# Block one's attention scores: from half-array fp32 products to whole-array fp32r products with high and low parts

## The chip, the cores and the metric

The kernel runs on one core of one Trainium2 chip. The metric is the device time of one execution in microseconds. Engines are named as in the profile: PE is TensorE (PEld its loads of the stationary operand), DVE is VectorE, ACT is ScalarE, POOL is GpSimd and SP issues most transfers.

## The reference, cut to what matters

The program is two transformer-like layers over 256 tokens of width 1024. Block one holds a sparse attention with 8 query heads of width 64, which share 2 key heads (4 query heads each). Each query head is scored three times: against 15 compressed keys, against the keys k_s of the selection branch, and against the keys k_w of the window branch.

```python
q = rms_norm(q.reshape(B_, S_, N_HEADS, HEAD_DIM), q_norm_g)
k_s = rms_norm(k_s.reshape(kv_shape), k_norm_g[1])
k_w = rms_norm(k_w.reshape(kv_shape), k_norm_g[2])
kc = rms_norm(compress(k_c.reshape(kv_shape), cmp_pos_k, w_cmp_k), k_norm_g[0])
...
s_c = (jnp.einsum('bsgrd,bcgd->bgrsc', q, kc) * SCALE - slopes * dist_c)      # compressed: 15 keys
...
s = (jnp.einsum('bqgrd,bgqmd->bgrqm', q_i, ks) * SCALE - slopes * dist)        # selection
s = (jnp.einsum('bqgrd,bkgd->bgrqk', q_i, k_i) * SCALE - slopes * dist)        # window
```

(The einsum texts are shortened; each is the product of one head's queries with its group's keys over the 64 head dimensions.) With 256 tokens the selection takes all blocks and the window reaches over all of them, so both branches are causal attention over all 256 keys with different keys and values.

## The kernel before, in words

Every large product is made from weights that are split in two: ACT writes the high part of a loaded unit of weights (2 k-tiles of 128x512, tile `whi`, type fp32r), DVE subtracts it from the loaded fp32 values and writes the low part (`wlo`, line 1787). PE adds three products per tile: high by high, high by low, low by high. Units follow one another in a fixed order (`b1_q`, `b1_kv`, `b1_w`, `b1_c0`, `b1_x0`, `b1_c1`, `b1_x1`, ...), and a ring of five buffers lies between the engines. The groups c0, x0, c1, x1 feed the convolution branch; their four tiles each are written by PE in banks 0 to 3, the left halves copied by ACT and the right halves added by DVE (`add_right`, line 2129, out `CC` or `UU`). Tile f of a group uses the same bank as tile f of the group before, so PE waits with the first product of tile f (`wait_bank`) for DVE's `add_right` of tile f in the group before.

Attention of block one is a side program, written as a generator on PE, ACT and DVE. Each engine takes one step `s` of it per unit, from the first unit of `b1_c0` on. The order on each engine is fixed by this text; nothing is scheduled otherwise.

- Step 1 to 3 on PE: the keys to be compressed (n = 0), the queries (n = 1, 2) and the keys k_s and k_w (n = 3) are turned into banks 4 and 5, head dimension on rows, two heads of 64 rows each.
- ACT copies them with their gains into `TT` (12 tiles of 128x256; steps 2 to 4). POOL then moves the keys by two transfers each so that each key head is there in both halves of the rows (`kc_swapped`, `ks_swapped`).
- DVE adds the position embedding into `KP` (steps 3 and 4), PE compresses the keys (step 5), ACT, DVE and POOL norm them (steps 6 and 7) and DVE writes them into `KCT`.
- Step 7 on PE: eight fp32 products give the compressed scores: 128 rows (two query heads, with zeros in `KCT` where head and key don't belong together) by 64 columns. DVE adds the bias (`CB`) to them in step 8.
- Steps 10, 13, 16, 19, 22, 26, 29, 32 on PE (`pair_at`): a pair is two query heads and one branch. The two heads stand in rows 0 to 63 and 64 to 127, so each product uses 64 rows of the array, and the two heads' products go to banks 4 and 5. Queries 0 to 127 meet 128 keys, queries 128 to 255 meet 256 keys: four fp32 instructions a pair. DVE (`negated`) takes the scores from there.

The lines of the trace: 523 is every product of PE, 527 every turn, 1174 every copy of ACT, 2010 `KP`, 2016 to 2029 the norm of the compressed keys, 2041 the bias.

## Time and profile before

| | us |
|---|---|
| median of 3 runs | 902.2 (902.16 to 902.3) |
| profiled execution | 901.26 |
| its span | 899.2 |
| PE busy | 892.7 (99%) |
| DVE busy | 706.0 (79%) |
| ACT busy | 555.3 (62%) |

The granted clock of PE was 0.999 of full speed in the profiled execution. PE is busy from end to end: the chain of work that ended last is PE for 99% of the span. A busy time of PE is made of overlapping records, so the price of a piece of PE's work is read from one start to the next start behind it. fp32 instructions leave two records each (two passes), fp32r instructions and turns one; the profile prints both types as f32.

### The profile page before, as it was taken

The numbers are of one execution on the slowest core, as the hardware profiler recorded it, in microseconds if no ns is written. First come the engines' busy times: TensorE is split into PE (matmuls) and PEld (weight loads), VectorE is DVE, ScalarE is ACT, GpSimd is POOL, SyncE is SP. The second block draws the span as 40 slices with busy tenths as digits, with TensorE's granted clock in tenths as the row PEclk, the third lists the DMA queues.
The fourth block names the chain that finished last, engine by engine and source line by source line (L and its number), as shares of the span: only waits on it lengthen the run. The fifth ranks groups of instructions, "written<-read, shape, count | busy, mean of one in ns | idle before, by whom it ended". The sixth has DMA issues, their size and how long they took to land.

```text
span 899.2 us, 13582 instructions
## 1 busy us (share of the span) xinstructions
PE 892.7 (99%) x4926; PEld 767.0 (85%) x4926; DVE 706.0 (79%) x1381; ACT 555.3 (62%) x954; POOL 43.2 (5%) x54
## 2 busy tenths in 40 slices
PE   9999999999999999999999999999999999999997
PEld 7988877888888888888889998888889988888886
DVE  6888899789866666677998999999976786666665
ACT  7767878755644444456655657776745755754454
POOL 0410000000000000000010100100000000000000
PEclk9999999999999999999999999999999999999999
DMA  9977677676465555556798888487565377555551
GB/s 343 320 214 199 177 203 219 198 293 202 154 229 187 192 191 196 190 191 209 219 236 268 231 206 270 106 230 240 169 211 164 114 212 237 187 187 187 188 188 47
DMA packets 97218, 184.53 MB, mean 205 GB/s; under 512 B 8128, under 2 KB 18176, under 8 KB 96896
## 3 DMA queue, kind: packets, MB, share of 16 engines
q1 hardware_dynamic: 92128, 166.35, 56.1%
q0 software_dynamic: 4656, 16.78, 10.0%
q8 instruction: 40, 0.66, 0.3%
q10 hardware_dynamic: 368, 0.52, 0.2%
q14 instruction: 26, 0.21, 0.1%
HBM read 164.69 MB, written 1.05 MB: 184 GB/s over the span
## 4 chain that ended last, share of the span: by engine, by line
PE 99%; ACT 1%; issue 0%; DVE 0%; DVEq 0%; ACTq 0%
PE pb L523 97%; PE pb L527 1%; PE pb L738 1%; ACT SM L1400 0%; ACT wlo L1174 0%; ACT SM L1174 0%; ACT whi L1174 0%; ACT PTC L1174 0%; DVE XS L2617 0%; DVE XS L2625 0%; DVEq L59 0%; DVE DG L2359 0%; ACT MSQ L1757 0%; DVE ST L2603 0%; ACT CC L1174 0%
## 5 line engine op out<-in xcount | busy, mean ns | idle before, releaser
L1174 ACT ACTIVATE whi<-raw 128x1024 fp32r<-128x1024 f32 (+2 forms) x304 | 309.1, 1039 | 125.5 <-PE pb L523 112.5
L1787 DVE TENSOR_TENSOR wlo<-raw,whi 128x1024 fp32r<-128x1024 f32 (+1 forms) x267 | 315.7, 1211 | 78.7 <-ACT whi L1174 78.2
L523 PE MATMUL pb<-XT,whi 128*128 128x512 f32 (+1 forms) x1232 | 283.8, 358 | 0.0
L523 PE MATMUL pb<-whi,ZO 128*128 128x512 f32 (+1 forms) x776 | 238.9, 388 | 0.0
L523 PEld LDWEIGHTS pb<-XT,whi 128*128 128x128 f32 x1232 | 200.8, 189 | 23.8 <-issue 1.4
L523 PEld LDWEIGHTS pb<-whi,ZO 128*128 128x128 f32 x776 | 145.2, 188 | 29.7 <-issue 0.4
L523 PE MATMUL pb<-XT,wlo 128*128 128x256 f32 (+1 forms) x1032 | 166.4, 282 | 0.0
L523 PEld LDWEIGHTS pb<-XT,wlo 128*128 128x128 f32 (+1 forms) x1032 | 153.2, 190 | 14.0
L523 PE MATMUL pb<-whi,XT 128*128 128x512 f32 (+1 forms) x544 | 161.8, 389 | 0.0
L523 PE MATMUL pb<-wlo,ZO 128*128 128x512 f32 (+1 forms) x388 | 148.3, 387 | 0.0
L523 PEld LDWEIGHTS pb<-whi,XT 128*128 128x128 f32 x544 | 101.0, 188 | 20.7 <-issue 0.7
L523 PE MATMUL pb<-wlo,XT 128*128 128x512 f32 (+1 forms) x272 | 95.8, 384 | 0.0
L2291 DVE SCALAR_TENSOR_TENSOR YC<-U,PR,YC 128x255 f32<-128x255 f32 (+14 forms) x240 | 94.9, 462 | 0.0
L523 PEld LDWEIGHTS pb<-wlo,ZO 128*128 128x128 f32 x388 | 72.9, 188 | 14.3
L2186 DVE TENSOR_TENSOR HF<-pb,RT 128x256 f32<-128x256 f32 x64 | 26.8, 419 | 43.1 <-ACT RT L1174 43.1
L523 PEld LDWEIGHTS pb<-wlo,XT 128*128 128x128 f32 x272 | 51.1, 188 | 9.8
L1174 ACT ACTIVATE RT<-pb 128x256 f32<-128x256 f32 x64 | 22.5, 374 | 55.0 <-PE pb L523 55.0
L1174 ACT ACTIVATE ZO<-HF 128x256 fp32r<-128x256 f32 x64 | 26.8, 418 | 31.1 <-DVE HF L2189 29.4
L1174 ACT ACTIVATE wlo<-raw 128x1024 fp32r<-128x1024 f32 x31 | 32.7, 1055 | 13.5 <-PE pb L523 13.5
L2664 POOL DMA_DIRECT2D wlo<-raw x31 | 26.9, 867 | 289.3 <-ACT wlo L1174 289.3
L2071 DVE STREAM_TRANSPOSE PT<-SM 32x192 f32<-32x192 f32 x80 | 29.5, 369 | 1.1
L2189 DVE SCALAR_TENSOR_TENSOR HF<-HF 128x256 f32<-128x256 f32 x64 | 27.2, 425 | 2.2
(258 smaller groups left out, 657.9 us busy)
## 6 DMA issues: line engine op xcount, KB each, us to landing
raw<-in_w_in SPq DMA_DIRECT2D x105, 512.0 KB, 4.8
raw<-in_w_ff SPq DMA_DIRECT2D x64, 512.0 KB, 5.3
raw<-in_w_up SPq DMA_DIRECT2D x32, 512.0 KB, 4.5
raw<-in_w_down SPq DMA_DIRECT2D x32, 512.0 KB, 4.8
wlo<-raw POOLq DMA_DIRECT2D x31, 512.0 KB, 5.8
raw<-in_w_branch_b SPq DMA_DIRECT2D x8, 512.0 KB, 5.3
raw<-in_w_out SPq DMA_DIRECT2D x8, 512.0 KB, 4.1
raw<-in_wx_kv SPq DMA_DIRECT2D x8, 512.0 KB, 5.4
```

Of the source, the lines that this page charges most:

```text
L523: return e.matmul(o, l, r, start=start, stop=stop, skip_group_check=True)
L527: return e.transpose(o, s, ident[0:n, 0:n])
L738: i = e.matmul(PB[4 + j][:, k * 256 + t * P:k * 256 + t * P + P], src[:, c:c + P], ident, start=k + t == 0, stop=k + t == 2, is_transpose= ...
L1174: return e.activation(o, i, ACT.Copy, scale=scale)
L1787: e.tensor_tensor(wlo[u % NW][:, 0:c], raw_tile(u)[:, 0:c], whi[u % NW][:, 0:c].bitcast(F32), ALU.subtract).then_inc(lo, 1)
L2071: i = e.transpose(PT2[n % 2][b:b + 32, :, a:a + 32], SM2[n % 2][a:a + 32, :, b:b + 32])
L2186: e.tensor_tensor(HF[:, f, :], PB[bank_of[name, f]][:, 0:256], RT[:, m % 2, :], ALU.add).then_inc(out_d, 1)
L2189: e.scalar_tensor_tensor(out=HF[:, f, :], in0=HF[:, f, :], scalar=0.0, in1=HF[:, f, :], op0=ALU.max, op1=ALU.mult).then_inc(h_sq, 1)
L2291: m = e.scalar_tensor_tensor(out=y, in0=U2[:, f, 30:256 + k], scalar=prm("convw2", 8 * k + f), in1=y, op0=ALU.mult, op1=ALU.add)
L2664: e.dma_start(wlo[u % NW][:, 0:c].bitcast(F32), raw_tile(u)[:, 0:c], accum_op=ALU.add).then_inc(lo_summed[u % NW], 16)
```

## The change

Each head's queries are kept as a high part (fp32r) in one half of the rows and their low part in the other half, 128 rows in all, in the columns of `OT` (`q_cols`, the right half of tile `ZO`; written there before attention's outputs come). The keys' high parts stand in both halves of the rows (`k_cols(g, 0, b)`), and so do their low parts (`k_cols(g, 1, b)`). A head's scores are then two fp32r products over all 128 rows, one with the keys' high part and one with their low part; all four partial products are summed. For this

- ACT's copies (n = 1 to 3) are made by halves of 64 rows: 12 instead of 6;
- DVE makes the low parts (`qk_low`, a new function, 4 instructions each in steps 3, 4 and 5), reading banks 4 and 5 again;
- PE's turn of n = 3 waits for `qk_low(1)`, which reads the bank that it writes;
- POOL moves the keys after `qk_low(3)`, by 2 transfers of 256 KB (`ks_doubled`) instead of 2 of 128 KB;
- a pair is 8 fp32r instructions instead of 4 fp32 ones;
- the compressed keys are treated alike (`KCS`): 16 fp32r products of 32 columns (16 high, 16 low) instead of 8 fp32 ones of 64 columns; DVE writes two tiles in step 7 and adds both products to the bias, which is loaded straight into `PC`, by 8 small instructions instead of 2 in step 8. The zeroing of `KCT` on POOL is gone.

Left out below: semaphore names, tile sizes and the zeroing.

```diff
...
+
+KCS = ZT[:, 0:64]
+
+def q_cols(f, p):
+    return slice(512 * f + 256 * p, 512 * f + 256 * p + 256)
+
+def k_cols(g, l, b):
+    a = 2048 + 1024 * g + 512 * l + 256 * b
+    return slice(a, a + 256)
...
-TQ, TK, TC = 0, 4, 8
-
-def key_tile(first_tile, w, g, half):
-    return first_tile + w + 2 * (g != half)
+def qk_gain(n, j, r):
+    a = PRM["kg"] + 1 + j
+    return PR[r, a:a + 1] if n == 3 else QG[r, 2 * n - 2 + j:2 * n - 1 + j]
+
+def key_tile(w, g, half):
+    return w + 2 * (g != half)
...
-            e.dma_start(CB[:, :], A["consts2"]).then_inc(cb_in, 16)
+            e.dma_start(PC[:, :], A["consts2"][:, 0:512]).then_inc(cb_in, 16)
+            e.dma_start(CB[:, 512:1024], A["consts2"][:, 512:1024]).then_inc(cb_in, 16)
         if u == b1 + 51:
...
-                    e.wait_ge(qk_out, n - 1)
+                    e.wait_ge(*((kc_copied, 1) if n == 2 else (qk_lo, 1)))
                 for j in range(2):
...
-                e.wait_ge(qk_out, 3)
+                e.wait_ge(qk_lo, 2)
+                kcs = KCS.rearrange("p (l n) -> p l n", l=2)
                 for t in range(2):
...
-                        a = 256 * t + 64 * f
-                        i = mm(PB[7][:, a:a + 64], TT[:, TQ + f, t * P:t * P + P], KCT[:, :],
-                               t == 0 and f == 0, t == 1 and f == 3)
+                        for p in range(2):
+                            a, g = 256 * t + 64 * f + 32 * p, f // 2
+                            i = mm(PB[7][:, a:a + 32].rearrange("p (l n) -> p l n", l=2),
+                                   OT[:, q_cols(f, p)][:, t * P:t * P + P], kcs[:, :, 15 * g:15 * g + 16],
+                                   a == 0, a == 480)
                 i.then_inc(cs_done, 1)
...
-                f, k = n // 2, [key_tile(TK, n % 2, n // 4, p) for p in range(2)]
-                e.wait_ge(qk_out, 4)
-                e.wait_ge(ks_swapped, 32)
+                f, b, g = n // 2, n % 2, n // 4
+                e.wait_ge(qk_lo, 3)
+                e.wait_ge(ks_doubled, 32)
                 if n:
...
-                    r = slice(64 * p, 64 * p + 64)
-                    mm(PB[4 + p][:, 0:128], TT[r, TQ + f, 0:128], TT[r, k[p], 0:128], True, False)
-                for p in range(2):
-                    r = slice(64 * p, 64 * p + 64)
-                    mm(PB[4 + p][:, 128:384], TT[r, TQ + f, 128:256], TT[r, k[p], 0:256], False,
+                    q = OT[:, q_cols(f, p)]
+                    mm(PB[4 + p][:, 0:128], q[:, 0:128], OT[:, k_cols(g, 0, b)][:, 0:128], True, False)
+                    mm(PB[4 + p][:, 0:128], q[:, 0:128], OT[:, k_cols(g, 1, b)][:, 0:128], False, False)
+                    mm(PB[4 + p][:, 128:384], q[:, 128:256], OT[:, k_cols(g, 0, b)], False, False)
+                    mm(PB[4 + p][:, 128:384], q[:, 128:256], OT[:, k_cols(g, 1, b)], False,
                        True).then_inc(sc_done, 1)
...
-                i0 = (TC, TQ, TQ + 2, TK)[n]
                 e.wait_ge(qk_t, n + 1)
...
-                    copy(TT[:, i0:i0 + 2, :].rearrange("p i n -> p (i n)"), PB[4][:, :]).then_inc(qk_out, 1)
-                else:
-                    if n < 3:
-                        e.wait_ge(qg_made, 1)
-                    g = [prm("kg", 1 + j) if n == 3 else QG[:, i0 + j - TQ:i0 + j - TQ + 1] for j in range(2)]
-                    copy(TT[:, i0, :], PB[4 + n % 2][:, 0:256], g[0])
-                    copy(TT[:, i0 + 1, :], PB[4 + n % 2][:, 256:512], g[1]).then_inc(qk_out, 1)
+                    copy(TT[:, 0:2, :].rearrange("p i n -> p (i n)"), PB[4][:, :]).then_inc(kc_copied, 1)
+                    continue
+                if n < 3:
+                    e.wait_ge(qg_made, 1)
+                for j in range(2):
+                    for p in range(2):
+                        r = slice(64 * p, 64 * p + 64)
+                        o = OT[r, q_cols(2 * n - 2 + j, p) if n < 3 else k_cols(p, 0, j)]
+                        i = copy(o, PB[4 + n % 2][r, 256 * j:256 * j + 256], qk_gain(n, j, r))
+                i.then_inc(qk_hi, 1)
             if s == 6:
...
-                e.wait_ge(kc_zero, 3)
+                e.wait_ge(kc_zero, 2)
                 step(copy(KC[0:30, 0:64], PB[7][0:30, 0:64]))
...
+    def qk_low(n):
+        e.wait_ge(qk_hi, n)
+        for j in range(2):
+            for p in range(2):
+                r, q = slice(64 * p, 64 * p + 64), slice(64 - 64 * p, 128 - 64 * p)
+                c = q_cols(2 * n - 2 + j, p) if n < 3 else k_cols(p, 0, j)
+                o = OT[q, c] if n < 3 else OT[r, k_cols(p, 1, j)]
+                i = e.scalar_tensor_tensor(out=o, in0=PB[4 + n % 2][r, 256 * j:256 * j + 256],
+                                           scalar=qk_gain(n, j, r), in1=OT[r, c].bitcast(F32),
+                                           op0=ALU.mult, op1=ALU.subtract)
+        i.then_inc(qk_lo, 1)
+
     def attention1():
...
+            if s in (3, 4, 5):
+                qk_low(s - 2)
             if s in (3, 4):
-                e.wait_ge(*((qk_out, 1) if s == 3 else (kc_swapped, 32)))
+                e.wait_ge(*((kc_copied, 1) if s == 3 else (kc_swapped, 32)))
                 for w in range(2):
...
-                        v = TT[r, key_tile(TC, w, g, half), 16 * half:16 * half + 240].rearrange(
+                        v = TT[r, key_tile(w, g, half), 16 * half:16 * half + 240].rearrange(
                             "p (c j) -> p c j", j=16)
...
-                e.wait_ge(kc_zero, 3)
+                e.wait_ge(kc_zero, 2)
                 step(e.tensor_scalar(KCN[0:30, :].rearrange("p (q d) -> p q d", q=2),
...
-                    i = e.transpose(KCT[32 * b:32 * b + 32, 32 * (b // 2):32 * (b // 2) + 32],
-                                    KCN[0:32, 32 * b:32 * b + 32])
+                    i = e.transpose(KCT[32 * b:32 * b + 32, :], KCN[0:32, 32 * b:32 * b + 32])
                 step(i)
...
-                e.tensor_scalar(KCT[:, :], KCT[:, :], prm("kg"), None, ALU.mult).then_inc(kct_out, 1)
+                step(e.tensor_scalar(KCS[:, 0:32], KCT[:, :], prm("kg"), None, ALU.mult))
+                after_step()
+                e.scalar_tensor_tensor(out=KCS[:, 32:64], in0=KCT[:, :], scalar=prm("kg"),
+                                       in1=KCS[:, 0:32].bitcast(F32), op0=ALU.mult,
+                                       op1=ALU.subtract).then_inc(kct_out, 1)
             pcv = PC[:, :].rearrange("p (h n) -> p h n", n=32)
...
-                e.wait_ge(cb_in, 16)
-                for p in range(2):
-                    d = PC[:, :].rearrange("p (t q n) -> p t q n", t=2, q=2)[:, :, p, :]
-                    b = CB[:, 0:512].rearrange("p (t q n) -> p t q n", t=2, q=2)[:, :, p, :]
-                    step(e.tensor_tensor(
-                        d.rearrange("p t (f n) -> p t f n", f=4),
-                        PB[7][:, :].rearrange("p (t f q n) -> p t f q n", t=2, f=4, q=2)[:, :, :, p, :],
-                        b.rearrange("p t (f n) -> p t f n", f=4), ALU.add))
+                e.wait_ge(cb_in, 32)
+                pc = PC[:, :].rearrange("p (t q f n) -> p t q f n", t=2, q=2, f=4)
+                cs = PB[7][:, :].rearrange("p (t f q l n) -> p t f q l n", t=2, f=4, q=2, l=2)
+                for l in range(2):
+                    if l:
+                        after_step()
+                    for g in range(2):
+                        for q in range(2):
+                            d = pc[:, :, q, 2 * g:2 * g + 2, 15 * g:15 * g + 15]
+                            step(e.tensor_tensor(d, cs[:, :, 2 * g:2 * g + 2, q, l, 0:15], d, ALU.add))
                 after_step()
...
-    for n, i, done in ((1, TC, kc_swapped), (4, TK, ks_swapped)):
-        e.wait_ge(qk_out, n)
-        e.dma_start(TT[64:128, i + 2:i + 4, :], TT[0:64, i:i + 2, :]).then_inc(done, 16)
-        e.dma_start(TT[0:64, i + 2:i + 4, :], TT[64:128, i:i + 2, :]).then_inc(done, 16)
+    e.wait_ge(kc_copied, 1)
+    e.dma_start(TT[64:128, 2:4, :], TT[0:64, 0:2, :]).then_inc(kc_swapped, 16)
+    e.dma_start(TT[0:64, 2:4, :], TT[64:128, 0:2, :]).then_inc(kc_swapped, 16)
+    e.wait_ge(qk_lo, 3)
+    for g in range(2):
+        r, q = slice(64 * g, 64 * g + 64), slice(64 - 64 * g, 128 - 64 * g)
+        k = OT[:, 2048 + 1024 * g:3072 + 1024 * g].bitcast(F32)
+        e.dma_start(k[q, :], k[r, :]).then_inc(ks_doubled, 16)
     e.wait_ge(kc_mean, 1)
...
```

DVE around step 3, before the change and after (`ZO` is the tile with the high and low parts, `KP` the keys with their positions, `CC` the right halves of group c0; line 2017 of the changed kernel is `qk_low`):

```order
L1787 TENSOR_TENSOR wlo<-raw,whi 128x1024 [waits w_hi_made] x2
L2010 TENSOR_TENSOR KP<-TT,PR 64x240 [waits qk_copied]
L2010 TENSOR_TENSOR KP<-TT,PR 64x240 x3
L2129 TENSOR_TENSOR CC<-pb,CC 128x256 [waits left_halves_copied] x4
L1787 TENSOR_TENSOR wlo<-raw,whi 128x1024 [waits w_hi_made]
```

```order
L1804 TENSOR_TENSOR wlo<-raw,whi 128x1024 [waits w_hi_made] x2
L2017 SCALAR_TENSOR_TENSOR ZO<-pb,ST,ZO 64x256 [waits qk_hi_made]
L2017 SCALAR_TENSOR_TENSOR ZO<-pb,ST,ZO 64x256 x3
L2041 TENSOR_TENSOR KP<-TT,PR 64x240 [waits cmp_keys_copied]
L2041 TENSOR_TENSOR KP<-TT,PR 64x240 x3
L2165 TENSOR_TENSOR CC<-pb,CC 128x256 [waits left_halves_copied] x4
L1804 TENSOR_TENSOR wlo<-raw,whi 128x1024 [waits w_hi_made]
```

Four instructions stand now ahead of `KP` and of the four `add_right` of c0.

PE at the first pair (step 10), before the change and after (`TT` and `ZO` hold queries and keys; `XT` and `wlo`, `whi` belong to the main stream):

```order
L523 MATMUL pb<-XT,wlo 128x256 x7
L523 MATMUL pb<-TT 128x128 [waits keys_swapped,qk_copied]
L523 MATMUL pb<-TT 128x128
L523 MATMUL pb<-TT 128x256 x2
L523 MATMUL pb<-XT,whi 128x512 [waits turned_lo,w_lo_made,w_hi_made]
```

```order
L535 MATMUL pb<-XT,wlo 128x256 x7
L535 MATMUL pb<-ZO 128x128 [waits keys_doubled,qk_lo_made]
L535 MATMUL pb<-ZO 128x128
L535 MATMUL pb<-ZO 128x256 x2
L535 MATMUL pb<-ZO 128x128 x2
L535 MATMUL pb<-ZO 128x256 x2
L535 MATMUL pb<-XT,whi 128x512 [waits turned_lo,w_lo_made,w_hi_made]
```

The place in the stream is the same; four instructions on two half arrays became eight on the whole array.

## Rows read from the trace of the kernel before

**Rows 1.** The page: PE's busy time; shares of the chain that ended last, by engine.

```profile
PE 892.7 (99%) x4926; PEld 767.0 (85%) x4926; DVE 706.0 (79%) x1381; ACT 555.3 (62%) x954; POOL 43.2 (5%) x54
...
PE 99%; ACT 1%; issue 0%; DVE 0%; DVEq 0%; ACTq 0%
```

**Rows 2.** Window 40:50: length; busy PE, PEld, DVE, ACT, POOL; clock, DMA share, GB/s.

```profile
40.00:50.00 10.00, 10.00 (x65) 8.97 (x64) 8.95 (x16) 7.59 (x15) 1.97 (x4) 1.00 0.89 281
```

**Rows 3.** Timeline of PE, 42 to 44 us: start, duration, line, operation, count.

```profile
42.59 1.11 PE L523 MATMUL pb<-XT,wlo 128*128 128x256 f32 x8
43.54 0.60 PE L527 MATMUL pb<-CST,QKV 128*128 128x128 f32 x4
```

**Rows 4.** Timeline of PE, steps 3 to 8 of attention.

```profile
46.78 0.60 PE L527 MATMUL pb<-CST,QKV 128*128 128x128 f32 x4
47.14 0.71 PE L523 MATMUL pb<-XT,whi 128*128 128x512 f32 x2
...
52.88 2.01 PE L523 MATMUL pb<-WC,KP 128*30 128x64 f32 x64
...
60.51 1.90 PE L523 MATMUL pb<-KCT,TT 128*128 128x64 f32 x16
62.21 0.71 PE L523 MATMUL pb<-XT,whi 128*128 128x512 f32 x2
```

**Rows 5.** Timeline of PE around the first pair.

```profile
69.72 1.11 PE L523 MATMUL pb<-XT,wlo 128*128 128x256 f32 x8
70.77 0.93 PE L523 MATMUL pb<-TT 64*128 64x128 f32 x8
71.62 0.72 PE L523 MATMUL pb<-XT,whi 128*128 128x512 f32 x2
72.19 0.40 PE L523 MATMUL pb<-XT,wlo 128*128 128x256 f32 x2
```

**Rows 6.** Timeline of PE: an fp32 product of 256 columns over 128 rows.

```profile
24.93 0.59 PE L523 MATMUL pb<-DR,CST 128*128 128x256 f32 x2
...
25.60 0.40 PE L523 MATMUL pb<-wlo,XT 128*128 128x512 f32 x1
```

**Rows 7.** Timeline of DVE, 41 to 74 us.

```profile
41.86 2.35 DVE L1787 TENSOR_TENSOR wlo<-raw,whi 128x1024 fp32r<-128x1024 f32 x2
44.13 1.65 DVE L2010 TENSOR_TENSOR KP<-TT,PR 64x240 f32<-64x240 f32 x4
45.79 1.33 DVE L2129 TENSOR_TENSOR CC<-pb,CC 128x256 f32<-128x256 f32 x3
...
48.35 1.23 DVE L1787 TENSOR_TENSOR wlo<-raw,whi 128x1024 fp32r<-128x1024 f32 x1 [0.52 <-ACT whi L1174]
...
55.56 0.14 DVE L2016 TENSOR_SCALAR ST<-ST 30x1 f32<-30x1 f32 x1 [1.34 <-ACT KCN L1366]
...
57.71 0.26 DVE L2029 TENSOR_SCALAR KCT<-KCT,PR 128x64 f32<-128x64 f32 x1
...
59.13 0.43 DVE L2129 TENSOR_TENSOR UU<-pb,UU 128x256 f32<-128x256 f32 x1 [0.82 <-ACT UU L1174]
...
63.45 0.75 DVE L2041 TENSOR_TENSOR PC<-pb,CB 128x256 f32<-128x256 f32 x2
...
69.94 0.18 DVE L2059 TENSOR_TENSOR ST<-ST 128x16 f32<-128x16 f32 x1
...
73.10 0.42 DVE L2129 TENSOR_TENSOR CC<-pb,CC 128x256 f32<-128x256 f32 x1
```

**Rows 8.** Timeline of DVE: two low parts of 128x256.

```profile
12.35 0.88 DVE L2365 SCALAR_TENSOR_TENSOR XT<-XG,XT 128x256 fp32r<-128x256 f32 x2
```

**Rows 9.** Timeline of ACT: query copies and the next high part.

```profile
41.01 0.83 ACT L1174 ACTIVATE TT<-pb,ST 128x256 f32<-128x256 f32 x2
41.73 1.07 ACT L1174 ACTIVATE whi<-raw 128x1024 fp32r<-128x1024 f32 x1
```

**Rows 10.** Timeline of PE: the first tile of x1.

```profile
74.51 0.63 PE L523 MATMUL pb<-XT,whi 128*128 128x512 f32 x2
```

## What is predicted

> **What bounds the kernel now.** I read the page first: PE is busy for 892.7 of 899.2 us and makes 99% of the chain that ended last [rows 1]. So the time is PE's own work, and the change is worth what it takes from PE's stream less each wait that it puts into it. ACT and DVE cost nothing until PE waits for them. The windows show where that is near: from 40 to 50 us, where the queries and keys are copied, DVE is busy 8.95 of 10 us [rows 2], and the change gives DVE more work just there. So I read PE's timeline for the price of each product by the distance of starts, then DVE's timeline for the slack between its work and PE's waits.
>
> **PE, the pairs.** Before, a pair takes 70.77 to 71.62 = 0.85 us. The group ahead of it (eight products of 256 columns) takes 69.72 to 70.77 = 1.05, while the same group ahead of a turn takes 42.59 to 43.54 = 0.95, so entering a pair costs 0.10 more. Behind it the first two products of 512 columns take 71.62 to 72.19 = 0.57, where four times 0.119 (a price worked out below) would be 0.48, so leaving it costs 0.1 [rows 3, 5]. Together 0.95 a pair, and 1.05 where the main stream follows at once, which it does behind the first pair.
>
> The new pair is eight whole-array fp32r products: four of 256 columns, at 0.95/8 = 0.119 each [rows 3], and four of 128 columns. No row shows an fp32r product under 256 columns. Bounds: the compressed scores are 16 passes of 64 columns in 60.51 to 62.21, so 0.106 each [rows 4]. Their columns are few, so this is the price of loading 128 stationary columns; each new product needs such a load as well. On the other side, an fp32 product of 256 columns and the 512-column product behind it take 24.93 to 25.60 = 0.67 [rows 6]; less 0.23 for the latter (the eight products at the fp32r pace of 0.119 per 256 columns give it) that is 0.44, or 0.22 for 128 columns at the fp32 rate. Below, a product of 128 columns that costs by its columns alone would take some 0.06, half of 0.119. I take 0.107, since the compressed scores are the nearest row: many passes, few columns, all 128 rows. A pair is then 4 x 0.119 + 4 x 0.107 = 0.90, with no entry cost since the array is used as by its neighbours. Eight pairs save 8 x 0.05 plus 0.1 at the first: **-0.5 us**. With 0.22 a pair is 1.36 and the eight cost 8 x 0.41 - 0.1 = +3.2; with 0.06 a pair is 0.72 and they save 8 x 0.23 + 0.1 = 1.9.
>
> What the pairs give up is that two heads run beside each other on half arrays. The Trainium skill, page "TensorE: Matmul & The Clock Gate", section "LDWEIGHTS (loading the stationary operand)", says that a load takes as long as it has columns, whatever its rows: 107 ns for 128 by its formula. By that rule, the trace agrees. Its section "Back-to-back issue gap" gives some 81 ns for a sustained product of 128 columns with its load; by that a pair would be 0.80 and the pairs would save 1.3 in place of 0.5, which is an estimate from that page. The 0.106 of the row speaks against it, and I go by the row.
>
> **PE, the compressed scores.** Eight fp32 products leave 16 passes of 0.106; 16 fp32r products of 32 columns need 16 loads too. At the price of a load: **0**. If few columns made them cheap (0.06), -0.7; even at the fp32 rate 32 columns stay below 0.106.
>
> **ACT.** Six copies of 128x256 become twelve of 64x256; the number of columns is the same, so each costs what one costs now, about 0.36 from start to start (41.01 to 41.73 for two [rows 9]). Before unit 18's high part that is +0.7: it ends at 43.5 instead of 42.8. DVE would have begun its low part at 43.0 (41.86 and half of the two), so DVE is 0.55 late. Later copies lie in ACT's idle time.
>
> **DVE, first wait.** `qk_low(1)` is four instructions of 256 columns; the nearest rows are two such low parts in 0.88, 0.40 from start to start [rows 8]. Four are 1.6. So `KP`, before at 44.13, starts 0.55 + 1.6 = 2.15 later, and so does `add_right` of c0's tile 0, before at 45.79 [rows 7]: it starts at 47.95 and ends near 48.4. PE's first product of x0 writes that bank and started at 47.14 [rows 4]; it had 0.9 of slack, and now comes at 48.45: **+1.3 us**. Tiles 1 to 3 follow at 0.34 on DVE and at 0.7 on PE and wait no more. The turn of n = 3 (46.78 [rows 4]) needs `qk_low(1)`, ended at 46.4: no wait of its own.
>
> **DVE, what follows.** The four adds end at 49.3 and the next low part, before at 48.35 behind a pause, starts there: the lateness is 1.0. It takes 1.14, `qk_low(2)` 1.6 and the second `KP` 1.65 as the first, so `KP` ends near 53.7, and PE wants it at 52.88 + 1.3 = 54.2. With `qk_low(3)` the lateness is 1.0 + 3.2 = 4.2, less the pause of 1.34 before 55.56: the norm's first instruction moves to 58.4. From there to the end of `KCT` it took 57.71 + 0.26 - 55.56 = 2.4 [rows 7], now with one small instruction and POOL's transfers before it 2.7: 61.1, and PE wants it at 60.51 + 1.3 = 61.8 [rows 4]. Both hold, by 0.5 and 0.7. Then DVE goes on without a pause to `add_right` of c1. The adds of x0, before at 59.13, start at 61.4, 2.25 late. The bias, before two instructions in 0.75, becomes eight small ones and one wait; each like the 128x16 row of 0.18, say 0.14 from start to start: +0.4. So c1's tile 0, before at 73.10, starts at 75.75 and ends at 76.15 [rows 7]. PE's first product of x1, which writes its bank, stood at 74.51 [rows 10]; with 1.3 of delay and 0.15 saved at the first pair it would come at 75.65. A second wait: **+0.5**. Behind 76 us DVE has idle time again and catches up.
>
> `ks_doubled` is issued near 57 and twice as large as before; the first pair is at 70.77. The change's two loads for one on SP move the same bytes. Both 0.
>
> **Sum.** -0.5 + 0 + 1.3 + 0.5 = +1.3 us. The profiled execution took 901.26 us for a span of 899.2, so it would take 902.6; the median of the runs is 0.9 above it, so I predict **903.5 us**. PE is the chain up to the end, so nothing behind gives a delay back. What a measurement here can't tell from no change is 0.2%, 1.8 us.
>
> **Rivals.**
>
> *Narrow fp32r products run at the fp32 rate* (slower). Price 0.22 for each of 4 x 8 products of 128 columns: pairs +3.2 instead of -0.5. The place is each pair's two 128-column halves, from the first pair on; it decides as soon as a product under 256 columns costs over 0.15. As PE then comes later to x1, the second wait shrinks to 0.1. 902.2 + 3.2 + 1.3 + 0.1 = 906.8. For it: no fp32r product in this kernel has fewer than 256 columns, so no row excludes it. Against it: in the rows a product costs by its columns or by its load, and none shows a third price.
>
> *Loads don't bound fp32r* (faster or none). 0.06 for a narrow product: -1.9 and -0.7 against waits of 1.8 and up to 0.8 more, since PE comes earlier to them: 902.2. Against it: 0.106 a pass in rows 4.
>
> *DVE isn't late*: the four instructions cost less than 0.25 each or fall in idle time, and PE waits for nothing. Then -0.5: 901.7. Against it: DVE's timeline has no gap from 41.86 to 47.
>
> **How the numbers follow.** My forecast 0.43, the fp32 rate 0.35, cheap loads 0.10, no lateness 0.12. The forecast's own range is 902.7 to 905: the waits may be twice what I worked out, as each hangs on sums of small durations. From 901.3 (below the rivals that gain) to 907.2 (the fp32 rate with somewhat longer waits) holds 0.8. Faster by over 0.2% means under 900.4, which needs cheap loads and no waits, or a gain that I don't see: 0.08. Slower by over 0.2% means over 904.0: all of the fp32 rate and about a quarter of my case, 0.46. The rest, 0.46, is the same.
>
> **What would show it.** A pair of 0.90 from start to start, PE's first product of x0 right behind the end of DVE's add of c0's tile 0 with an idle gap of about 1.3 on PE, a gap of half a microsecond before x1, and 16 compressed products in 1.7. A pair over 1.2 would be the fp32 rate; one near 0.72, or compressed products in under 1.2, cheap loads. The forecast is wrong if PE starts x0 on time, or if it waits elsewhere: for `KP`, for `KCS`, or for the doubled keys.

## The result and the profile after

| | before | after |
|---|---|---|
| median of 6 runs each on one chip, us | 902.15 (901.48 to 902.3) | 906.92 (905.95 to 907.47) |
| profiled execution | 901.26 | 906.88 |
| its span | 899.2 | 904.8 |

The ratio is 1.0057, 95% interval 1.0046 to 1.0068: slower by 4.8 us. It lies inside the stated range and outside the 902.7 to 905 of my own forecast. 906.8 is also what the rival of the fp32 rate gave, so the first question is whether its mechanism is at work. The page of the changed kernel:

```profile
PE 894.2 (99%) x4926; PEld 770.3 (85%) x4926; DVE 712.3 (79%) x1400; ACT 558.4 (62%) x960; POOL 42.9 (5%) x53
...
PE 93%; DVE 4%; DMA 1%; issue 1%; ACT 1%; SPq 0%; POOL 0%; DVEq 0%; ACTq 0%
```

PE's busy time grew by 1.5 us only [rows 1]. The chain tells where the rest is: PE gave up 6% of it, and DVE, which had 0%, holds 4%. PE's timeline (start, duration, line, operation; in brackets the idle time ahead, and what ended it):

```profile
49.41 0.63 PE L539 MATMUL pb<-CST,QKV 128*128 128x128 f32 x4 [1.63 <-DVE ZO L2017]
51.65 0.70 PE L535 MATMUL pb<-XT,whi 128*128 128x512 f32 x2 [1.61 <-DVE CC L2165]
...
57.39 2.03 PE L535 MATMUL pb<-WC,KP 128*30 128x64 f32 x64
...
65.04 1.87 PE L535 MATMUL pb<-ZO 128*128 128x32 f32 x16
66.76 0.71 PE L535 MATMUL pb<-XT,whi 128*128 128x512 f32 x2
...
74.26 1.12 PE L535 MATMUL pb<-XT,wlo 128*128 128x256 f32 x8
75.22 1.09 PE L535 MATMUL pb<-ZO 128*128 128x128 f32 x8
76.14 0.63 PE L535 MATMUL pb<-XT,whi 128*128 128x512 f32 x2
76.61 0.39 PE L535 MATMUL pb<-XT,wlo 128*128 128x256 f32 x2
...
80.32 0.70 PE L535 MATMUL pb<-XT,whi 128*128 128x512 f32 x2 [1.23 <-DVE CC L2165]
...
106.28 1.16 PE L535 MATMUL pb<-ZO 128*128 128x128 f32 x8
107.37 0.87 PE L535 MATMUL pb<-PT,QKV 128*64 128x256 f32 x8
```

The narrow products are not dear: 16 of 32 columns go from 65.04 to 66.76, 0.107 each, and a pair from 75.22 to 76.14, 0.92. The fp32 rate would be 1.36. The time is in three idle stretches: ahead of the turn of n = 3, of x0 and of x1.

This execution was already 0.85 late at the turn of step 1 (it starts at 40.73; 39.88 in the profiled execution of before), ahead of everything that the change adds to PE, ACT and DVE. In the nine further executions below this turn starts between 39.93 and 40.67. No kernel was profiled twice, so how much of the 0.85 is chance stays open. I take it off: the two executions then differ by 5.6 - 0.85 = 4.8, as the medians do. That is in part luck, as the profiled execution of before was 0.9 under its median (901.26 against 902.15) and the changed kernel's was not. The turn of n = 3 is late by 49.41 - 0.85 - 46.78 = 1.8, x0 by 51.65 - 0.85 - 47.14 = 3.66 [rows 4], x1 by 80.32 - 0.85 - 74.51 = 4.96 [rows 10]. DVE shows what PE waited for:

```profile
46.03 1.23 DVE L1804 TENSOR_TENSOR wlo<-raw,whi 128x1024 fp32r<-128x1024 f32 x1 [1.23 <-ACT whi L1189]
47.29 1.98 DVE L2017 SCALAR_TENSOR_TENSOR ZO<-pb,ST,ZO 64x256 fp32r<-64x256 f32 x4
49.30 1.66 DVE L2041 TENSOR_TENSOR KP<-TT,PR 64x240 f32<-64x240 f32 x4
50.97 1.42 DVE L2165 TENSOR_TENSOR CC<-pb,CC 128x256 f32<-128x256 f32 x4
...
69.59 1.23 DVE L2080 TENSOR_TENSOR PC<-pb,PC 128x60 f32<-128x60 f32 x8
...
79.64 1.41 DVE L2165 TENSOR_TENSOR CC<-pb,CC 128x256 f32<-128x256 f32 x4
```

The four low parts take 47.29 to 49.30, 0.50 each; the turn starts at their end. The adds of c0 start at 50.97, later than before by 50.97 - 0.85 - 45.79 = 4.3 [rows 7]; I had 2.15. The other half is ahead of the low parts: DVE waits 1.23 us for ACT's high part. ACT's timeline:

```profile
40.41 2.22 ACT L1189 ACTIVATE whi<-raw 128x1024 fp32r<-128x1024 f32 x2 [1.08 <-DMA raw<-in_w_in]
...
43.01 1.90 ACT L1189 ACTIVATE ZO<-pb,ST 64x256 fp32r<-64x256 f32 x4
44.94 1.06 ACT L1189 ACTIVATE whi<-raw 128x1024 fp32r<-128x1024 f32 x1
```

Two things: four copies take 43.01 to 44.94, 0.48 each where I had 0.36, and ACT itself waited 1.08 us for weights at 39.3, which it did not in the profiled execution of before. Whether that wait belongs to the change was the next question.

### The profile page after: what moved, and what is told of

The parts are those of the page before. It is cut to its first block, busy times and chain, and to the rows that moved or that the text cites. A ratio compares the mean times of both kernels' runs of the same rounds, so it can differ in the third digit from the quotient of the medians.

```text
span 904.8 us, 13607 instructions
## 1 busy us (share of the span) xinstructions
PE 894.2 (99%) x4926; PEld 770.3 (85%) x4926; DVE 712.3 (79%) x1400; ACT 558.4 (62%) x960; POOL 42.9 (5%) x53
## 3 DMA queue, kind: packets, MB, share of 16 engines
HBM read 164.69 MB, written 1.05 MB: 183 GB/s over the span
## 4 chain that ended last, share of the span: by engine, by line
PE 93%; DVE 4%; DMA 1%; issue 1%; ACT 1%; SPq 0%; POOL 0%; DVEq 0%; ACTq 0%
PE pb L535 91%; DVE wlo L1804 1%; PE pb L750 1%; DMA raw<-in_w_in 1%; PE pb L539 1%; DMA raw<-in_w_first 1%; DVE ZO L2017 1%; DVE KP L2041 0%; ACT ZO L1189 0%; DVE CC L2165 0%; ACT whi L1189 0%; DVE UU L2165 0%; SPq L464 0%; DVE QKV L2008 0%; DVE CC L2144 0%
```

## The experiments

The theory was: PE's products cost what they cost before, and all of the loss is ACT's and DVE's added instructions ahead of the adds that free PE's banks. The rivals: the narrow products or the change of array use cost something after all; the later transfers come from the change. Ratios are to the kernel before, run beside each.

**Without the low parts, and one half after the other.** In the first kernel `qk_low` is gone and its rows are zeroed once; in the second the loops over tile and half change places in ACT's copies and in `qk_low`; the third (below) has both.

```diff
-            if s in (3, 4, 5):
-                qk_low(s - 2)
```
```diff
-                for j in range(2):
-                    for p in range(2):
+                for p in range(2):
+                    for j in range(2):
```

> The changed kernel without DVE's twelve instructions for the low parts of queries and keys; POOL zeroes the tile early instead, so the scores leave out the low parts of queries and keys (those of the compressed keys are still made). PE's products, ACT's copies by halves and POOL's transfers stay. Theory A (PE waits for the low parts, and for what DVE does behind them): the waits of 1.6 and 1.6 us at steps 3 and 4 and of 1.2 before x1 shrink to at most 0.5 together, pairs stay at 0.92, and the time is 901.7 to 902.7. Theory B (narrow fp32r products are dear): the time stays over 905. Theory C (ACT's copies by halves, 1.2 later, are what PE waits for): x0 still starts 1 us or more late, 903.5 or more.

Measured: 902.58 us, ratio 1.0012 [1.0003, 1.0021]. All of PE's products are there, and one wait is left ahead of x0:

```profile
48.58 0.70 PE L535 MATMUL pb<-XT,whi 128*128 128x512 f32 x2 [0.55 <-DVE CC L2165]
```

PE waits nowhere ahead of x1 either. It is 1.44 late at x0 (48.58 against 47.14 [rows 4]) and 1.6 at the end of the span (900.8 against 899.2), so all of its narrow products behind x0 cost what they replaced within 0.2 us. Both rivals about PE's stream fall. One thing stays open: four of the 11 executions took 903.5 to 904.2, the others 901.9 to 902.8, and the profiled one (902.84) is not among the four.

> The changed kernel with the loops over half and column block exchanged in ACT's copies and in the low parts, so that of four instructions two in a row work on the same 64 rows, where all alternated. Theory A1 (an instruction on the other half of the rows begins only when the one before has written; one on the same rows overlaps it by 0.1): four copies take some 1.7 in place of 1.9 and four low parts 1.8 in place of 2.0; the first waits shrink by 0.4 to 0.7 and the time is 906.0 to 906.6. Rival A2 (64 rows or the fp32r output make it, not the alternation): spacing stays 0.48 and 0.50, time 906.9.

Measured: 904.37 us, 1.0032 [1.0020, 1.0045]: a gain of 2.2 us, more than expected, from the order of the same instructions. ACT, DVE and PE:

```profile
41.34 1.66 ACT L1189 ACTIVATE ZO<-pb,ST 64x256 fp32r<-64x256 f32 x4
```
```profile
45.38 1.78 DVE L2017 SCALAR_TENSOR_TENSOR ZO<-pb,ST,ZO 64x256 fp32r<-64x256 f32 x4
```
```profile
49.53 0.70 PE L535 MATMUL pb<-XT,whi 128*128 128x512 f32 x2 [1.60 <-DVE CC L2165]
...
77.79 0.70 PE L535 MATMUL pb<-XT,whi 128*128 128x512 f32 x2 [0.83 <-DVE CC L2165]
```

Four copies take 1.66 in place of 1.90 and four low parts 1.78 in place of 1.98. Instructions that alternate between the two halves of the rows stand apart by more than those that stay in one: here ACT's four copies start at 41.34, 41.70, 42.17 and 42.54, 0.36 apart within a half and 0.47 from one half to the other. The row of `KP` said so before the change: its four instructions alternate, the last ended 1.65 us behind the first one's start and the next instruction began at 1.66, so spacing and duration are the same 0.41 [rows 7]. Two low parts over 128 rows stood 0.40 apart and took 0.88 together, so each lasts 0.48 and they overlap [rows 8]. The gain is larger than 0.24 + 0.20 a step, and three steps stand in a row: x1's wait shrank by 0.4, and the turn of n = 3 is hardly late any more. But this profiled execution (904.24) also had its weights in time. Three of the five executions lie at 904.2 to 904.4 like it, the other two at 905.7 and 906.0. So how much of the 2.2 is the order, and how much that more executions had their weights in time, these runs don't tell; the shorter groups are shown, 2.2 us as their price is not.

**The turn's wait taken away.** The turn of n = 3 writes bank 6 and no longer waits for DVE (ACT and DVE read that bank then):

```diff
-                        if n >= 2:
-                            e.wait_ge(*((kc_copied, 1) if n == 2 else (qk_lo, 1)))
+                        if n == 2:
+                            e.wait_ge(kc_copied, 1)
...
-                                i = turn(PB[4 + n % 2][:, ...
+                                i = turn(PB[6 if n == 3 else 4 + n % 2][:, ...
```

> The changed kernel with the turn of the keys (n = 3) into bank 6 instead of 5, so that PE's turn waits for no low part. Theory A says that the wait for the turn (1.6) only moves: PE is held by DVE's add of c0's tile 0, which ends at the same time, but the turn's 0.36 of work and its wait's tail lie before it: gain 0.2 to 0.6, time 906.3 to 906.7. Rival (both waits add up, so one less is 1.6 to 1.8 less): 905.2.

Measured: 906.44 us, 1.0053 [1.0040, 1.0065]. PE's timeline, and windows of 2 us (length; busy PE, PEld, DVE, ACT, POOL; granted clock, DMA share, GB/s):

```profile
50.64 0.70 PE L535 MATMUL pb<-XT,whi 128*128 128x512 f32 x2 [2.80 <-DVE CC L2165]
```
```profile
48.00:50.00 2.00, 0.00 (x0) 0.00 (x0) 1.91 (x6) 1.96 (x4) 0.00 (x0) 1.00 1.04 324
50.00:52.00 2.00, 1.36 (x6) 1.21 (x7) 2.00 (x5) 1.95 (x4) 0.00 (x0) 0.87 0.34 123
52.00:54.00 2.00, 2.00 (x8) 1.71 (x8) 1.94 (x4) 0.14 (x1) 0.00 (x0) 0.50 0.25 30
54.00:56.00 2.00, 2.00 (x10) 1.63 (x10) 1.90 (x6) 0.68 (x1) 0.00 (x0) 0.77 0.65 237
```
```profile
78.67 1.22 DVE L2165 TENSOR_TENSOR CC<-pb,CC 128x256 f32<-128x256 f32 x3
```

The two waits became one of 2.80: the first did not add to the second. Counted from the turn of step 1, x0 starts at 50.64 - 40.35 = 10.29, where the changed kernel has 51.65 - 40.73 = 10.92: a gain of 0.6. That the median lies in the expected range is luck all the same, as the windows show something that I had not looked for. Behind the pause the granted clock falls to 0.50, which is 1.2 GHz. What it costs is read from one start to the next: from x0 to the compression of the keys PE takes 57.94 - 50.64 = 7.30, and 57.39 - 51.65 = 5.74 in the changed kernel, so 1.56 more. In the changed kernel's profiled execution the clock stays at 1.00 behind its two pauses of 1.6 us. In return the wait ahead of x1 is gone: DVE's add of c1's tile 0 begins at 78.67 and takes 0.42, and PE, held up by its clock, comes at 79.48. So the fall of the clock took the place of the second wait and hardly lengthened the run. Two of the changed kernel's own six executions have a mean granted clock of 0.995, as low as the 0.996 here, and took 907.3 and 907.5, only 0.4 to 0.6 over the median.

**The kernel before with the split transfer.** One load of constants as two, nothing else:

```diff
-                    e.dma_start(CB[:, :], A["consts2"]).then_inc(cb_in, 16)
+                    e.dma_start(CB[:, 0:512], A["consts2"][:, 0:512]).then_inc(cb_in, 16)
+                    e.dma_start(CB[:, 512:1024], A["consts2"][:, 512:1024]).then_inc(cb_in, 16)
```

> The kernel before with its second table of constants loaded by two transfers of 256 KB instead of one of 512 KB, as in the changed kernel. In the changed kernel's profile ACT waited 3.2 and 1.1 us for weights at 35 and 40 us. If the split did that: 902.7 to 903.3. If it was the chance of that execution: 902.2, within 0.3 of before.

Measured: 901.63 us, 0.9998 [0.9989, 1.0007]. ACT, DVE and PE:

```profile
39.66 2.22 ACT L1175 ACTIVATE whi<-raw 128x1024 fp32r<-128x1024 f32 x2 [1.12 <-DMA raw<-in_w_in]
```
```profile
46.87 1.42 DVE L2130 TENSOR_TENSOR CC<-pb,CC 128x256 f32<-128x256 f32 x4
```
```profile
47.56 0.70 PE L524 MATMUL pb<-XT,whi 128*128 128x512 f32 x2
```

The weights are 1.12 late here too and the adds of c0 1.1 later than in rows 7, and PE's product of x0 only 0.4 (47.14 in [rows 4]). I find the late weights at this place in 8 of the 11 profiled executions, of kernels with the change and without it; before, and the experiments with one half after the other and with the late low parts, had none. So the split of this load does not make it, and the one execution of before that I read was among the few without it. With late weights the 0.9 us of slack ahead of x0 are gone.

**The kernel before with the low parts.** It makes them and uses none; the turn of n = 3 waits for the first four, the first pair for all. ACT's copies are those of before.

```diff
+            if s in (3, 4, 5):
+                qk_low(s - 2)
```

> The kernel before with the twelve instructions of the low parts added to DVE at the same places (steps 3, 4 and 5) and PE's turn of n = 3 waiting for the first four, as in the changed kernel; what they write is used by nothing. ACT's copies, PE's products and the transfers are those of before. Theory A (DVE's added work is what PE waits for): PE waits before x0 (1.0 to 1.8 together with the turn) and before x1 (0.8 to 1.3), time 903.6 to 904.8. Theory B (it is PE's new products): 902. Rest of the loss against the changed kernel would then be ACT's slower copies.

Measured: 904.91 us, 1.0036 [1.0023, 1.0050]: DVE's added work by itself makes 3.1 of the 4.8 us, with what PE's clock did behind it. DVE and PE:

```profile
45.28 1.98 DVE L2008 SCALAR_TENSOR_TENSOR ZO<-pb,ST,TT 64x256 fp32r<-64x256 f32 x4
47.29 1.65 DVE L2026 TENSOR_TENSOR KP<-TT,PR 64x240 f32<-64x240 f32 x4
48.95 1.42 DVE L2145 TENSOR_TENSOR CC<-pb,CC 128x256 f32<-128x256 f32 x4
```
```profile
49.63 0.70 PE L523 MATMUL pb<-XT,whi 128*128 128x512 f32 x2 [1.60 <-DVE CC L2145]
```
```profile
77.16 0.42 DVE L2145 TENSOR_TENSOR CC<-pb,CC 128x256 f32<-128x256 f32 x1
```

A pause of 1.60 ahead of x0, and behind it again a granted clock of 0.63 and 0.52 in the two windows of 50 to 54 us: from x0 to the compression of the keys 7.31 in place of 5.74, 1.57 more. The wait ahead of x1 that I expected is not there. DVE's add of c1's tile 0 ends at 77.58 and PE comes at 78.57; without the fall of the clock PE would have come at about 77.0 (my estimate, 78.57 - 1.57) and would have waited. So this run doesn't tell whether the low parts alone bring a second wait.

**Neither low parts nor alternating halves.**

> As e1_no_lows (no low parts of queries and keys in the scores, the tile is zeroed early), with ACT's copies in the order of e2_same_half. Four copies take 1.66 instead of 1.90; if the wait of 0.55 before x0 in e1_no_lows was ACT's slower copies, it shrinks by about 0.3 and the time is 902.2 to 902.4; if ACT has no part in it, 902.6 again. Below 901.5 only if the pairs gain more than the 0.4 that their rows show.

Measured: 902.36 us, 1.0006 [0.9997, 1.0015], one wait of 0.50 ahead of x0. With both causes taken out the time is 0.6 us over that of before, and the interval includes no difference.

**The low parts later.** They stand behind `KP` in steps 4 and 5 and behind the norm's mean in step 6, so that nothing new of DVE's is ahead of c0's adds; the turn of n = 3 goes to bank 6, and POOL does its part of the norm ahead of its transfers. The second kernel has one half after the other as well.

```diff
-            if s in (3, 4, 5):
-                qk_low(s - 2)
...
+            if s in (4, 5):
+                qk_low(s - 3)
...
                         ALU.mult, ALU.add).then_inc(kc_mean, 1)
+                qk_low(3)
```

> The changed kernel with the keys turned into bank 6 and the low parts made later on DVE: the first four behind the second KP in step 4, the next in step 5, the last in step 6 where DVE waited for POOL, with POOL's norm ahead of its transfers. Theory A: the wait before x0 falls to the 0.5 to 0.8 of e1_no_lows, but 5 us of the low parts now press on the compressed keys and on x1: new waits of 1 to 2 there, 903.4 to 904.4. Rival (only the place before x0 matters, the rest has room): 902.6 as e1_no_lows.

Measured: 906.85 us, 1.0055 [1.0043, 1.0068]; expected 903.4 to 904.4. PE and DVE:

```profile
63.34 1.93 PE L535 MATMUL pb<-ZO 128*128 128x32 f32 x16 [1.78 <-issue]
```
```profile
59.18 1.97 DVE L2017 SCALAR_TENSOR_TENSOR ZO<-pb,PR,ZO 64x256 fp32r<-64x256 f32 x4
61.18 0.42 DVE L2145 TENSOR_TENSOR CC<-CC,RX 128x256 f32<-128x256 f32 x1
61.53 0.27 DVE L2052 TENSOR_SCALAR KCN<-KC,ST 30x128 f32<-30x128 f32 x1
61.83 0.85 DVE L2057 STREAM_TRANSPOSE KCT<-KCN 32x32 f32<-32x32 f32 x4
...
62.99 0.25 DVE L2062 SCALAR_TENSOR_TENSOR ZO<-KCT,PR,ZO 128x32 fp32r<-128x32 f32 x1
```

PE isn't late at x0, and then waits at the compressed scores: DVE's last write of the compressed keys ends at 63.24, PE starts at 63.34. The trace names no releaser; the two times do. `qk_low(3)` stands in that chain. The granted clock is 0.53 and 0.61 in the two windows of 66 to 70 us: from the product behind the compressed scores to the first pair PE takes 10.02 (65.12 to 75.14), where the changed kernel takes 8.46, another 1.56.

> e7_late_lows with the order of halves of e2_same_half: each group of four instructions 0.24 shorter on ACT and 0.2 on DVE, and the waits 0.4 to 0.8 shorter in all: 902.8 to 903.8. If it comes under 901.8, the products' gain of 0.4 shows and the version beats both.

Measured: 904.86 us, 1.0039 [1.0026, 1.0051]; expected 902.8 to 903.8. Three small waits, 1.05 ahead of x0, 0.85 at the compressed scores and 1.23 ahead of x1, and no fall of the clock. My expectation of both was wrong in the same way: DVE has hardly any room there (in these two executions it is idle for 2.7 and 2.1 of the 39 us from 41 to 80), so moved work comes out at the next wait.

**Off DVE and ACT, onto POOL.** ACT copies as before the change, the turn of n = 3 waits for ACT alone, and POOL splits:

```diff
+                for j in range(2):
+                    for p in range(2):
+                        ...
+                        chained(e.tensor_copy(OT[r, c], TT[r, 2 + 2 * n + j, :]))
+                        chained(e.tensor_tensor(o, TT[r, 2 + 2 * n + j, :], OT[r, c].bitcast(F32), ALU.subtract))
```

> The changed kernel, with the added copies and low parts taken off both busy engines: ACT copies queries and keys in fp32 over 128 rows, two instructions a turn, as before the change; POOL, which has under 8 us of work between 40 and 85 us, makes the high part (a copy) and the low part (a subtraction) from ACT's copy, 24 instructions of 64 rows, one after the other. The turn of n = 3 waits only for ACT. Theory (PE's products cost nothing more, all of the loss is ACT's and DVE's added instructions in front of c0's adds): no wait before the turn, x0 or x1 beyond 0.5 us, 901.4 to 902.6, no slower than the kernel before. What can spoil it is POOL's own pace, which no run shows for 64 rows by 256 columns: under 0.8 us an instruction the first 16 end by 56 us and nothing waits; at 1.2 us they end after 61 us, and PE waits at the compressed scores for the queries' low parts, or at the norm of the compressed keys: 904 to 908. Rival (the loss is in PE's stream, or in the transfers' bytes): 905 to 906.5 with no waits of PE on DVE.

Measured: 906.76 us, 1.0047 [1.0034, 1.0061]; missed. POOL, DVE and PE:

```profile
44.58 1.60 POOL L2689 TENSOR_TENSOR ZO<-TT,ZO 64x256 fp32r<-64x256 f32 x1
46.24 0.46 POOL L2688 CAST ZO<-TT 64x256 fp32r<-64x256 f32 x1
46.78 0.77 POOL L2689 TENSOR_TENSOR ZO<-TT,ZO 64x256 fp32r<-64x256 f32 x1
...
58.50 0.74 POOL L2689 TENSOR_TENSOR ZO<-TT,ZO 64x256 fp32r<-64x256 f32 x1
```
```profile
45.51 2.83 DVE L2026 TENSOR_TENSOR KP<-TT,PR 64x240 f32<-64x240 f32 x4
48.36 1.42 DVE L2150 TENSOR_TENSOR CC<-pb,CC 128x256 f32<-128x256 f32 x4
49.69 1.60 DVE L1803 TENSOR_TENSOR wlo<-raw,whi 128x1024 fp32r<-128x1024 f32 x1
```
```profile
49.04 0.70 PE L536 MATMUL pb<-XT,whi 128*128 128x512 f32 x2 [1.29 <-DVE CC L2150]
...
73.28 1.22 PE L536 MATMUL pb<-XT,wlo 128*128 128x256 f32 x8 [0.99 <-DMA wlo<-raw]
...
78.88 0.70 PE L536 MATMUL pb<-XT,whi 128*128 128x512 f32 x2 [0.67 <-DVE CC L2150]
```

POOL was quick enough, mostly (0.46 and 0.77 an instruction, the queries done at 59.2). But DVE lost time beside it: `KP` takes 2.83 where it takes 1.65 to 1.67 in every other kernel, and the low part behind the adds 1.60 in place of 1.22. The adds of c0, which read a bank and one tile, take 1.42 as always. The Trainium skill, page "SBUF — State Buffer", section "Who interferes with whom", says that a VectorE instruction with two inputs in SBUF contends with a GpSimd instruction that reads SBUF, as its second input comes through a shared interface. By that rule, the trace agrees: `KP` and `wlo` have two such inputs and grew, the adds have one and did not. At other times POOL was the one that lost: beside a low part of 1.21 at 54.53 its subtraction took 1.94. POOL's other duty suffered too. It starts the transfers that make low parts of some weights, one of them at 66.91 where the changed kernel starts it at 63.09, and PE waits 0.99 for it at 73.28. PE also waits 1.64 us for ACT at 87.73; I have not followed that one to its cause.

**What the waits explain.** For each profiled execution: PE's idle time in the window of 40 to 90 us (50 less the busy time), the time that the clock's fall cost (as read above), both less the 0.37 idle of before, and against it how much longer than before this same execution takes from the turn of step 1 to its end. The medians' differences to before stand beside it; they are of other executions.

| kernel | idle | clock | sum less 0.37 | same execution | medians |
|---|---|---|---|---|---|
| changed | 4.47 | 0 | 4.1 | 4.8 | 4.8 |
| no low parts | 0.85 | 0 | 0.5 | 0.9 | 0.8 |
| one half after the other | 2.47 | 0 | 2.1 | 2.8 | 2.6 |
| bank 6 | 3.10 | 1.6 | 4.3 | 4.7 | 4.7 |
| before, low parts | 2.12 | 1.6 | 3.3 | 4.1 | 3.1 |
| no low parts, one half after the other | 0.80 | 0 | 0.4 | 1.1 | 0.6 |
| late low parts | 2.22 | 1.6 | 3.4 | 4.1 | 5.0 |
| late, one half after the other | 3.13 | 0 | 2.8 | 3.5 | 3.1 |
| POOL splits | 4.60 | 0 | 4.2 | 5.7 | 5.0 |

In the first eight rows waits and clock leave 0.4 to 0.8 us, in the last 1.5. A part of that is how idle time is counted: the records in front of a pause overlap it. Ahead of x0 of the changed kernel the idle time is 1.61, but from the turn's start at 49.41, with its own 0.36 [rows 4], to 51.65 it is 1.88. The rest isn't settled. A profiled execution can also lie up to 1.0 beside its median, as for the late low parts (905.81 against 906.85), so single rows don't price a median. The row of the changed kernel is the sum to be explained:

```profile
40.00:90.00 50.00, 45.53 (x331) 40.29 (x330) 46.65 (x115) 35.82 (x78) 6.63 (x9) 1.00 0.76 211
```

No version came out under the kernel before; the nearest with the whole computation is 2.6 us over it.

## Why the prediction was wrong

The direction and the mechanism held: PE waits for DVE's adds of c0 ahead of x0, and again ahead of x1. The step that failed is the lateness of those adds, "2.15 later", and with it the +1.3 of the first wait: they came 4.3 later, and x0 3.66. The +0.5 ahead of x1 was too small for the same reason and measured 1.4. The sum, term by term (measured values from the two profiled executions, with the start's 0.85 taken off; the pairs' is what the others leave):

| term | predicted | measured |
|---|---|---|
| eight pairs | -0.5 | +0.1 |
| compressed scores | 0 | 0.02 |
| up to x0, the turn of n = 3 included | +1.3 | +3.66 |
| ahead of x1 | +0.5 | +1.4 |
| idle time ahead of a later turn, gone | not named | -0.4 |
| sum | +1.3 | +4.8 |

The idle time of before that is gone:

```profile
81.92 0.55 PE L527 MATMUL pb<-CST,SM 128*128 128x128 f32 x3 [0.37 <-ACT SM L1174]
```

*ACT's copies.* I gave a copy of 64 rows the 0.36 of one of 128 rows, by its columns. It took 0.48, as alternating halves don't overlap: 1.93 for four against 0.72 for two, +1.2 and not +0.7. Here the loss was half shown before: `KP` in rows 7 alternates as well, and its spacing was its duration.

*The low parts.* 0.50 each, not 0.40, for the same reason: 2.0 for four.

*The weights.* They came 1.1 late for ACT, in this execution as in most. The kernel before with them late (the split transfer) comes only 0.4 later at x0, so most of them falls into its slack; the change had already used that slack up. My 0.9 of slack was read from one execution that had them in time. The three parts are 0.5 + 0.4 + 1.1 = 2.0 of the 2.15 that I missed.

*The turn of n = 3.* "No wait of its own" was wrong: its low parts end at 49.27, with the start's 0.85 off at 48.4 and not at 46.4, and the turn is 1.8 late. But this wait doesn't add to the next: in bank 6 it is gone, x0's grows to 2.80, and x0 comes 0.6 earlier. For the most part it only shows half of the same lateness earlier.

*The second wait.* It was 1.4, not 0.5. The bias took 1.23 in eight instructions, near my 0.4 + 0.75. What I had too small is again the low parts, by 0.4 in each of two further steps, which is nearly all of the 0.9. Without the low parts this wait is absent, though the eight additions are there. Whether it needs the eight additions as well is not shown: in the kernel before with low parts, and in bank 6, it is absent too, but there PE's clock had already held PE up.

*The pairs.* A pair of 0.92 was right, and the first pair saved 0.12 (74.26 to 76.61 is 2.35; 69.72 to 72.19 was 2.47 [rows 5]). But I took this neighbourhood for all eight. Five pairs stand ahead of the products of attention's values, which have 64 columns: there the pair takes 106.28 to 107.37, 1.09, where it took 101.15 to 102.00, 0.85, before. Some of this comes back ahead of the pair, but each of the five loses about 0.06. My reading, which no run tests: changing to a part of the array costs, the kernel before paid for it at the pair, and now it is paid at these products. I had the place of the pairs from the first only.

*The rival of the fp32 rate.* I gave it 0.35, and its 906.8 is close by accident. Nothing of it is in the trace.

*The chances.* That a chain of small durations on a full DVE could be twice as long stood in the text, but priced to 905 only. The errors on DVE's chain all had one sign and added up: on an engine without idle time each underestimate is carried to the next wait.

## What to carry over

Slack that is read from one profiled execution is one sample: before a change is put into it, ask which waits for a transfer that execution happened not to have. Where an engine is full for tens of microseconds, work moved along it is not hidden, it comes out at the next wait, and splitting instructions into halves of the rows costs by itself, above all if they alternate; write one half's instructions and then the other's. A product that costs PE nothing still has to be fed: its operands' preparation is the price of such a change.

## What the runs showed of the hardware

- fp32r products of 32 columns over 128 rows cost 0.107 us each (16 in 1.72), as much as fp32 passes of 64 columns (0.106 [rows 4]). Between 32 and 64 columns their number does not show.
- Four copies of 64x256 on ACT take 1.90 us with alternating halves, 1.66 with one half after the other; four low parts on DVE 1.98 and 1.78.
- The granted clock fell to its lower level behind PE's pauses of 2.80, 1.60 and 1.78 us (bank 6, before with low parts, late low parts), and did not behind pauses of 1.63 and 1.61 (changed) and 1.60 (one half after the other). What decides it the runs don't tell. Where it fell, PE lost 1.56 us in each of the three; in bank 6 it replaced a wait ahead of x1 that made the changed kernel 1.4 late.
- With POOL's copies and subtractions beside it, DVE's `KP` took 2.83 us in place of 1.65.
